# A hybrid decoder step: the memory's scores among the last turns of the attention, the page numbers behind the first roots

## The reference

```python
s = jnp.einsum('bqhr,bkr->bhqk', ql, ckv) + jnp.einsum('bqhd,bkd->bhqk', qr, krope)      # attention over the prompt
s = jnp.where(kpos[None, :] <= qpos[:, None], s.astype(jnp.float32) * MLA_SCALE, NEG_INF)
pr = jax.nn.softmax(s, axis=-1).astype(ckv.dtype)
...
s = jnp.einsum('bshd,bmhd->bhsm', qh, mem_k).astype(jnp.float32) * (HEAD_DIM ** -0.5)    # attention to the memory
pr = jax.nn.softmax(s, axis=-1).astype(q.dtype)
```

## Time and profile before

| What | Value |
|---|---|
| device time, median of 3 runs | 3518.31 us (3515.1 to 3522.21) |
| the profiled execution: its own time | 3512.8 us |
| its span, first to last instruction | 3511.0 us |
| PE busy | 3400.2 us, 97% |
| DVE, ACT, POOL busy | 58%, 36%, 7% |
| chain that ended last, by engine | PE 86%, ACT 5%, DVE 4%, DMA 2% |
| TensorE's granted clock, mean | 0.997 of full speed |

### The profile page before, as it was taken

The page is one execution under the profiler, slowest core; times in us unless marked ns, Lnnn a source line. Parts: engine busy times, 40 slices in busy tenths (PEclk is TensorE's granted clock), DMA queues, the critical chain, the costliest instruction groups (busy, mean ns, idle before and its releaser), DMA issues.

```text
span 3511.0 us, 80468 instructions
## 1 busy us (share of the span) xinstructions
PE 3400.2 (97%) x33076; PEld 2591.2 (74%) x33076; DVE 2023.6 (58%) x5212; ACT 1267.0 (36%) x3599; POOL 243.9 (7%) x284
## 2 busy tenths in 40 slices
PE   7999999999999999999999999999999999999998
PEld 5768686877869678686567786868778687776864
DVE  3656565665656556565356566656656565464653
ACT  2323334242343423524433233332423434234343
POOL 3200100000010000000040001000000000000000
PEclk9999999999999999999999999999999999999999
DMA  7654453625436153252365634536263351632512
GB/s 218 208 175 158 144 189 108 200 88 184 135 122 206 51 200 123 102 192 69 106 216 174 201 127 173 155 115 210 63 231 115 117 186 49 236 110 91 194 55 68
DMA packets 281024, 514.82 MB, mean 147 GB/s; under 512 B 30037, under 2 KB 215571, under 8 KB 268115
## 3 DMA queue, kind: packets, MB, share of 16 engines
q1 hardware_dynamic: 258903, 463.96, 40.3%
q0 software_dynamic: 11648, 41.95, 3.4%
q10 hardware_dynamic: 10108, 3.76, 0.4%
HBM read 473.15 MB, written 47.49 MB: 148 GB/s over the span
## 4 chain that ended last, share of the span: by engine, by line
PE 86%; ACT 5%; DVE 4%; issue 2%; DMA 2%; DVEq 1%; ACTq 1%; POOL 0%; SPq 0%; POOLq 0%
PE bank L815 78%; PE bank L819 7%; DVEq L1548 1%; DMA win<-in_w_in 1%; DMA wout<-in_w_out 1%; ACT Q L2575 1%; ACT PT L2690 0%; ACT Sm L2645 0%; ACT qr L2574 0%; DVE mix L1778 0%; ACTq L2551 0%; ACT L2552 0%; ACT Q L2573 0%; DVE swaa L1776 0%; DVE mix L1774 0%
## 5 line engine op out<-in xcount | busy, mean ns | idle before, releaser
L815 PE MATMUL bank<-hT,win 128*128 128x256 f32 (+3 forms) x6384 | 1188.1, 339 | 5.4 <-DMA win<-in_w_in 2.7
L815 PEld LDWEIGHTS bank<-hT,win 128*128 128x128 f32 (+1 forms) x6384 | 949.2, 186 | 143.1 <-issue 34.7
L815 PE MATMUL bank<-wout,win 128*128 128x128 f32 x3136 | 379.9, 276 | 0.0
L815 PEld LDWEIGHTS bank<-wout,win 128*128 128x128 f32 x3136 | 364.6, 192 | 1.0
L815 PE MATMUL bank<-kv,Q 96*128 96x512 f32 (+3 forms) x640 | 276.4, 529 | 0.2
L1915 DVE TENSOR_REDUCE ml<-bank 128x1 f32<-128x512 f32 (+3 forms) x320 | 195.3, 610 | 124.1 <-PE bank L815 113.7
L819 PEld LDWEIGHTS bank<-cst,Sm 128*128 128x128 f32 x1344 | 157.6, 141 | 145.9 <-issue 67.4
L819 PE MATMUL bank<-cst,Sm 128*128 128x128 f32 x1344 | 210.7, 278 | 24.9 <-ACT Sm L2645 18.0
L2645 ACT ACTIVATE Sm<-bank,ml 128x512 f32<-128x512 f32 (+3 forms) x320 | 200.1, 626 | 76.8 <-DVE ml L1920 70.8
L815 PE MATMUL bank<-wout,mix 128*128 128x512 f32 x480 | 218.4, 605 | 2.2 <-DMA wout<-in_w_out 1.3
L815 PEld LDWEIGHTS bank<-wout,mix 128*128 128x128 f32 x480 | 89.8, 192 | 109.6 <-issue 107.9
(11 more groups left out here) (527 smaller groups left out, 5952.3 us busy)
## 6 DMA issues: line engine op xcount, KB each, us to landing
win<-wfast SPq DMA_DIRECT2D x98, 1024.0 KB, 6.7
win<-in_w_in SPq DMA_DIRECT2D x78, 1024.0 KB, 5.6
win<-wfast SPq DMA_DIRECT2D x98, 768.0 KB, 6.1
wout<-in_w_out SPq DMA_DIRECT2D x60, 512.0 KB, 7.8
out_xres<-xin SPq DMA_DIRECT2D x16, 1024.0 KB
win<-in_w_in SPq DMA_DIRECT2D x16, 896.0 KB, 4.9
PT<-in_w_out SPq DMA_DIRECT2D x28, 512.0 KB, 3.8
XX<-in_w_out SPq DMA_DIRECT2D x28, 512.0 KB, 4.6
```

The costliest lines, as they stand in the source:

```text
L815: return pe.matmul(out, lhsT, rhs, start=start, stop=stop, skip_group_check=True)
```

## The change

PE issues each half of the memory's scores among the last turns: half 0 behind turn n - 4, half 1 behind turn n - 2. They go to the banks which the next chunks of scores would have had (`freed_banks`), and the transposes of the inverse sums go to the fifth of these. DVE takes both maxima ahead of the sums and inverse sums. ACT's order is unchanged; it reads other banks. POOL's conversion of the page numbers stands behind its first roots and the roots of the first rows.

```diff
+        def freed_banks(m):
+            return [score_bank(8 * (m + 1) + i) for i in range(5)]
+        def memory_bank(m, j, h):
+            return freed_banks(m)[2 * j + h]
...
                     turn(c)
                     if c + 5 < n:
                         scores(c + 5)
+                    if c in (n - 4, n - 2):
+                        memory_scores(B, (c - n + 4) // 2)
                     if c > m and (c - m) % 4 == 0:
...
                 if B.prompt:
-                    memory_scores(B, 0)
-                    memory_scores(B, 1)
                     group_norm(B, 0)
                     tile(B, 25)
                     pe.wait_ge(s_on.h, s_on.at(B.ip, 1))
                     for i in range(4):
-                        last = tr(PP[5][:, i * P:(i + 1) * P], flat3(T3)[:, i * P:(i + 1) * P], P)
+                        last = tr(PP[freed_banks(B.m)[4]][:, i * P:(i + 1) * P], flat3(T3)[:, i * P:(i + 1) * P], P)
...
                     if B.turns and B.block and c > 5 and scaled < 8:
                         scale_rows(B, scaled)
                         scaled += 1
+                memory_max(B, 0)
+                memory_max(B, 1)
                 v.wait_ge(s_ae.h, n0 + n)
                 v.tensor_reduce(rsum, psum[:, :, 0:m + 1], AX, ADD)
...
                     scaled = attention(B, l, m, e)
-                    memory_max(B, 0)
-                    memory_max(B, 1)
                     centre(B)
...
-            pool.wait_ge(s_pg.h, 16 * 4)
-            pool.tensor_copy(pgf[:, :], pgi[:, :])
-            pool.drain()
-            pool.tensor_scalar(pgf[:, :], pgf[:, :], 4.0, K("sub"), MULT, ADD)
-            pool.drain()
...
                 x_roots(l * IT + 1)
+                if l == 0:
+                    pool.wait_ge(s_pg.h, 16 * 4)
+                    pool.tensor_copy(pgf[:, :], pgi[:, :])
+                    pool.drain()
+                    pool.tensor_scalar(pgf[:, :], pgf[:, :], 4.0, K("sub"), MULT, ADD)
+                    pool.drain()
                 for q in range(5):
```

More of the change, by code:

```diff
@@ L1240, in memory_scores @@
                     for p in range(2):
-                        last = mm(PP[6 * j + h][:, p * NM:(p + 1) * NM], mq[q, p, J], memKT[q, p, :])
+                        last = mm(PP[memory_bank(B.m, j, h)][:, p * NM:(p + 1) * NM], mq[q, p, J], memKT[q, p, :])
                 last.then_inc(s_ms.h, 1)
@@ L1246, in turn @@
                     pe.wait_ge(s_mn.h, s_mn.at(B.ip, j + 1))
-                    b0 = 6 * j
                     for q in range(4):
                         for t in range(2):
-                            last = tr(PP[b0 + q // 2][:, (q % 2) * T + t * P:(q % 2) * T + (t + 1) * P],
+                            last = tr(PP[memory_bank(B.m, j, q // 2)][:, (q % 2) * T + t * P:(q % 2) * T + (t + 1) * P],
                                       Pm[j][:, q, t * P:(t + 1) * P], P)
@@ L1947, in gate_attention @@
                     drain()
-                    v.tensor_tensor(x, x, halves(5, n), MULT).then_inc(s_uvr.h, 1)
+                    v.tensor_tensor(x, x, halves(freed_banks(B.m)[4], n), MULT).then_inc(s_uvr.h, 1)
                     return
@@ L1956, in memory_max @@
                 for h in range(2):
-                    v.tensor_reduce(top[:, 2 * h:2 * h + 2], halves(6 * j + h, T), AX, MAX)
+                    v.tensor_reduce(top[:, 2 * h:2 * h + 2], halves(memory_bank(B.m, j, h), T), AX, MAX)
                 drain()
@@ L2682, in block @@
                         for q in range(4):
-                            last = act.activation(Pm[j][:, q, :], PP[6 * j + q // 2][:, (q % 2) * T:(q % 2) * T + T], ACT.Exp,
+                            last = act.activation(Pm[j][:, q, :], PP[memory_bank(m, j, q // 2)][:, (q % 2) * T:(q % 2) * T + T], ACT.Exp,
                                                   bias=mst[j][1][:, q:q + 1], scale=MEM_SCALE, accum_out=mst[j][2][:, q:q + 1])
@@ L2689, in block @@
                         for q in range(2):
-                            last = act.activation(PTm[j][:, q, :, :], PP[6 * j + q][:, :].rearrange("p (a t) -> p a t", a=4), ACT.Copy)
+                            last = act.activation(PTm[j][:, q, :, :], PP[memory_bank(m, j, q)][:, :].rearrange("p (a t) -> p a t", a=4), ACT.Copy)
                         last.then_inc(s_mtr.h, 1)
```

## The result

The changed kernel takes 3497.62 us (median of five runs, 3495.08 to 3502.23), the kernel before beside it 3515.1 (3509.79 to 3522.21). The ratio is 0.995, with a 95% interval of 0.9934 to 0.9967. The forecast was 3496. The profiled execution took 3495.94 us, its span 3494.1 instead of 3511.0, so 16.9 less where the prediction had 22.1. I call this smaller difference the miss; most of what follows is about it.

What follows compares the result with a forecast made beforehand. PE is busy 3400.2 of 3511.0 us, so only its 110.8 us of standing still can be won. Start 5.1 plus last turns 17.0 make 22.1; 3518.3 - 22.1 gives 3496, range 3489 to 3505 (reaching 3488 to 3507 with rivals).

Steps and rivals of the forecast that it cites:

- The start: Kernel start: POOL's first root no longer waits for the page conversion, so PE begins 5.1 us earlier (3 to 7).
- The weights' slack of 0.6: Kernel start: the memory's weights land at 16.8, PE asks at 17.4; 0.6 us to spare, the smallest slack.
- The prediction's last rival: Kernel start: PE's clock rises before the first product, so the change wins 2 us more; 3492, chance 0.02.
- the slack of 2: Kernel start: ACT normalises the first rows of x until 27.96, PE asks at 30.0; slack 2 us.
- PE's work: Whole kernel: the change takes no work from PE, whose busy time stays at 3400 us.
- The last turns: End of each block's attention: halves of the memory's scores fill PE's waits for ACT; 8.5 us a layer, 17.0 in all.
- the price of a half: Last turns: a half of the memory's scores is 1.01 us of PE and wins at most that from the wait behind it.
- ACT's chain moves along: Last turns: ACT's next work depends on something behind half 0, which wins nothing; total gain 11.3 us, 3507, chance 0.06.
- The start gives nothing: Kernel start: the memory's weights land later or DMA issues hold POOL; only 17.0 us is left, 3501, chance 0.06.
- The wait is handed on: Behind the attention: the last turns' gain returns as PE's waits for centred squares or memory's probabilities; 3513, chance 0.05.
- Slower by the maxima: Behind the attention: two maxima, 2.9 us of DVE a block, delay inverse sums and `centre`; 3525, chance 0.03.

Runs made afterwards that it cites:

- the values first: Changed kernel with the halves of the memory's scores behind the same turn's values, not ahead: 3496.26 us in one run, later 3497.01 (five runs), ratio 0.9949.
- the half cut again: Changed kernel, but in blocks 4 and 5 the first two matmuls of half 1 stand behind turn n - 3, the others behind n - 2: 3500.72 us, one run.
- the split experiment: Kernel before with the mean's matmul put between the two halves of the memory's scores, making two runs of one: 3523.7 us, one run.

## Why the prediction came out right, and where it missed

**The number: in part luck.** 3496 stood 1.6 us from the 3497.62 measured, but two errors met in it. The median of the kernel before was taken as 3518.3 and came out as 3515.1, 3.2 lower; the gain was taken as 22.1 and came out as 3515.1 - 3497.62 = 17.5, 4.6 smaller. The gain lies in the range of 17 to 26, near its lower end.

**The start: right in the mechanism.** Predicted 5.1, measured 5.03 at the first transpose. At the first product of the projections it was 44.63 - 39.33 = 5.30. The weights' slack of 0.6 held here, but not in the run with only POOL's order changed. In the other profiles the first transpose came at 12.78 to 13.84 with the new order and at 17.98 to 18.49 with the old one: about 4.8 by their means, give or take half a microsecond from one execution to the next.

The clock makes more of a difference behind that. The prediction had PE start at the lower level, by the pace of its rows (the clock column shows 1.00 there, so the pace is all there is), and let this loss move along; in the kernel after it did, with 12.30 for 12.55. In four of the nine profiles with the new start (POOL's order alone, the values first in its first profile, the half cut again, and the kernel after beside the values first) the product took 10.5 to 10.6 us. The prediction's last rival has the change win 2 us more then. It didn't: these four begin the first projection at 38.76 to 41.18 and are sixty rows on at 53.84 to 56.03; the other five begin at 39.33 to 40.51 and are there at 52.79 to 53.96. What the product won went into PE's waits for the rows of x (up to 1.66, so the slack of 2 was used up) and for the normalised input, and into a stretch of 3.4 or 6.8 us at the lower level behind them. None of the three profiles with the old start has this stretch; why it comes stays open.

**PE's work: right.** 3402.6 against 3400.2 us.

**The last turns: the term was mis-sized, 17.0 for 14.1.** The step that missed is the price of a half, "(385.65 - 383.62)/2 = 1.01 us of PE". That is what it releases behind the attention, but not what it takes among the turns. Block 3 in the kernel after:

```profile
782.25 0.88 PE L827 MATMUL bank<-cst,Sm 128*128 128x128 f32 x5
...
783.06 1.14 PE L823 MATMUL bank<-memKT,mq 64*128 64x256 f32 x8
...
784.13 0.66 PE L827 MATMUL bank<-cst,Sm 128*128 128x128 f32 x4
...
786.39 0.66 PE L827 MATMUL bank<-cst,Sm 128*128 128x128 f32 x4
...
786.98 1.14 PE L823 MATMUL bank<-memKT,mq 64*128 64x256 f32 x8
788.05 0.66 PE L827 MATMUL bank<-cst,Sm 128*128 128x128 f32 x4
...
788.64 0.32 PE L823 MATMUL bank<-pr,kv 128*64 128x128 f32 x1
```

The last transpose of the five starts at 782.25 + 0.88 - 0.27 = 782.86, the first behind the half at 784.13. That is 1.27, and without the half it would be 0.11: a half costs 1.17 here (to rounding). Two cost 2.33 and release 2.03 behind the attention, so a block pays 0.30 for being split, which is the 0.31 of the split experiment. Each block's gain is then 2.03, less 2.33, plus the free time of PE that the halves fill:
- Block 2: half 0 fits wholly into its wait, 1.17, half 1 fills nothing. -0.30 + 1.17 = 0.87; measured 0.80, 0.81. The prediction had 1.01.
- Block 3: both waits of the earlier trace rows are gone. In the kernel before the first, shown for 0.75, was worth 788.34 - (786.38 + 1.21 - 0.27) - 0.11 = 0.91, and the wait for the copy, shown for 0.34, 792.05 - (790.61 + 1.09 - 0.27) - 0.20 = 0.42 (0.20, since the shape changes there). -0.30 + 0.91 + 0.42 = 1.03; measured 0.96; predicted 1.45. The 0.07 left over, here and in block 2, are perhaps the pace behind a half: four transposes there take 0.66, so they stand 0.13 apart, where in a group of eight it is (1.09 - 0.27)/7 = 0.12.
- Blocks 4 and 5: half 1 stands where PE goes from transposes to values, and that step costs 0.20 anyway (above: 788.64 - (788.05 + 0.66 - 0.27)), so a half costs 1.07 here. 2.03 - 1.17 - 1.07 + 1.17 = 0.96; measured 0.95 and 0.96. Predicted 1.01.
- Block 7: 1.45, predicted 1.54. Here the price of the split was nearly made up by free time that I had not counted: the kernel before has eight transposes in one group ahead of the two waits,

```profile
1684.09 1.37 PE L819 MATMUL bank<-cst,Sm 128*128 128x128 f32 x8
```

and at 0.11 apart they would take 0.27 + 7 x 0.11 = 1.04. The 0.33 more is a third short wait inside the group, which half 0 fills too. The other two, from start to start less 0.11, are 1686.10 - (1684.09 + 1.37 - 0.27) - 0.11 = 0.80 and 1687.26 - (1686.10 + 0.66 - 0.27) - 0.11 = 0.66. So -0.30 + 0.33 + 0.80 + 0.66 = 1.49.
- Block 6: 1.24 for 1.32, the same kind of place; I did not work it out by rows.
- Blocks 0 and 1: 0.15 and 0.52 for 0.39 and 0.77. The experiment with the values first gives the rest: in both, half 0 stood in ACT's chain. The prediction saw this for block 0 and took half 0 for worthless there; with the price of a split it is below worthless. In block 1 it counted nothing for half 0 either, without this reason.

PE in block 4, the kernel after:

```profile
998.44 1.14 PE L823 MATMUL bank<-memKT,mq 64*128 64x256 f32 x8
...
999.52 0.44 PE L827 MATMUL bank<-cst,Sm 128*128 128x128 f32 x2
...
1000.38 0.66 PE L827 MATMUL bank<-cst,Sm 128*128 128x128 f32 x4 [0.43 <-ACT Sm L2652]
...
1000.97 1.14 PE L823 MATMUL bank<-memKT,mq 64*128 64x256 f32 x8
...
1002.04 0.32 PE L823 MATMUL bank<-T,kv 128*64 128x128 f32 x1
```

Half 0 takes the first of the two waits of the earlier trace rows and part of the second, whose rest of 0.43 stays, as predicted.

**The rivals.** ACT's chain moves along: true of blocks 0 and 1 only. The start gives nothing: fell in the profiles, though the times of that part alone don't show it. The wait is handed on: fell; the mean of block 1 begins at 382.00 and the centred squares are there at 384.61, 2.6 behind it and 2.2 ahead of PE, as predicted:

```profile
382.00 1.12 PE L823 MATMUL bank<-cxs,cst 128*128 128x512 f32 x2
...
383.92 0.69 DVE L1888 TENSOR_TENSOR T<-cxs 128x512 f32<-128x512 f32 x1
...
386.85 1.02 PE L823 MATMUL bank<-T,cst 128*128 128x512 f32 x2
```

Slower by the maxima: fell. In their new place the squares come 2.2 us ahead of PE, no wait for `T3` came up, and the stretch up to the transposes of the inverse sums got shorter in every block. More, by the clock: its condition came in four profiles, and none of them had the gain sixty rows into the projection.

**The rest of the span.** Start and last turns give 5.3 + 14.1 = 19.4, the span fell by 16.9. The other 2.5 us can be placed by how far the kernel after is ahead at the same row. It is 5.30 ahead at the first projection, and from block to block the lead grows by the stretches, except at these places:
- Up to the attention of block 0 it falls from 5.30 to 177.65 - 173.00 = 4.65. The largest piece is a pause of PE in the recurrence which no wait explains: 0.47 before (132.12), 1.30 after (127.47). The other ten profiles show 0.38 to 1.53 there, and the two of them with the old start 0.75.
- At the end of block 0, 1.67 are lost: 373.18 - 370.05 = 3.13 at the attention of block 1, where 4.65 + 0.15 would be due. At the end of layer 1's first block 1.68 are won. Both are the granted clock, and they cancel.
- Behind block 5, 0.80 are lost, as the output weights are waited for 1.52 (1253.73) instead of 0.72 (1260.30); 0.20 come back a block later.
- Behind the last block's stretch, 1.09 are lost: the lead is 17.94 there and 16.85 at the end. From 16 us ahead of the end, the mean granted clock over 8 us is 0.57 where it was 0.79.

The third number from the right is the mean granted clock; first before, then after:

```profile
3495.00:3503.00 8.00, 5.15 (x24) 1.13 (x24) 2.09 (x14) 0.00 (x0) 0.00 (x0) 0.79 0.39 145
```

```profile
3478.00:3486.00 8.00, 6.07 (x24) 1.24 (x24) 1.45 (x8) 0.00 (x0) 0.00 (x0) 0.57 0.33 121
```

Together 0.65 + 1.67 - 1.68 + 0.60 + 1.09 = 2.3; the rest is in pieces of 0.14 and less.

Of the two places that cancel, the first lies behind a wait: at the end of block 0 PE waits 3.24 us for DVE in the kernel before, and 3.23 in the kernel after, and then the granted clock is at its lower level, 1.2 GHz, for a while. The timeline of PE, before and after:

```profile
206.68 0.81 PE L815 MATMUL bank<-kv,cst 128*128 128x8 f32 x6 [3.24 <-DVE kv L2001]
```

```profile
201.88 1.36 PE L823 MATMUL bank<-kv,cst 128*128 128x8 f32 x6 [3.23 <-DVE kv L2010]
```

A table of stretches of the kernel before has there, and at the same place of layer 1 (0.50 would be the lower level throughout):

```profile
207.00:212.00 5.00, 5.00 (x12) 2.33 (x12) 1.56 (x8) 0.00 (x0) 2.93 (x1) 0.66 0.98 399
1948.00:1952.00 4.00, 4.00 (x6) 1.54 (x5) 1.25 (x6) 0.00 (x0) 2.72 (x1) 0.57 1.01 418
```

and the same places of the kernel after

```profile
202.00:209.00 7.00, 7.00 (x14) 3.60 (x14) 2.97 (x13) 0.00 (x0) 2.93 (x1) 0.52 0.82 334
1938.00:1942.00 4.00, 4.00 (x10) 1.79 (x10) 0.94 (x6) 0.00 (x0) 2.93 (x1) 1.00 1.01 409
```

At the first place the level stayed low for 6.8 us, (1 - 0.52) x 2 x 7 to rounding, instead of 3.4; at the second it did not fall at all. These places differ as much between two profiles of one and the same kernel: the kernel after had at the first place 6.8 us here, and 3.4 in its two later profiles. None of these places is in the code that the change touches, but no run isolates any of them; whether the change has a part in the end's or the weights' loss stays open. 2.5 us is also within what runs of one kernel differ by (3495.08 to 3502.23), so the prediction's own range rightly had room for it.

## What to carry to other kernels

Work moved into a wait is not priced by its rows alone. Read from the last row ahead of it to the first row behind it, at its new place: where it has another shape than its neighbours, it pays for the change of shape (0.20 instead of 0.11 us ahead of it here), and cutting one run in two pays twice. Put such work where the shape changes anyway, and behind, not ahead of, what another engine's chain is waiting for. And don't cut a pair of matmuls that run side by side on the two halves of the array: a half of it takes as long as the whole.

## What the hardware showed that I had not expected

- A step from one shape of matmul to another on PE takes 0.20 us where rows of one shape and 128 columns follow 0.11 apart, and the step is not shown as idle time of PE. One more run of 64-row matmuls cost 0.31 us, sixteen times over.
- Rows of 64 with 256 columns, in pairs on both halves of the array, take 1.07 us for eight; four of one half alone take 1.06.
- The clock's lower level behind the same wait lasted 3.4 or 6.8 us, or didn't come, in executions of the same code. 3.4 us more or less of it moved what follows by 1.7 us.
- PE's faster pace in its first product came in four of nine executions with the new start and won nothing: each of them was then at the lower level for 3.4 or 6.8 us behind its next waits.
